# Neighbourhood attention with tokens by grid column, and hand-overs between engines reordered, in a two-block transformer kernel

## The reference, cut to what matters

```python
x = x + g1 * o_lat                                            # layers 0 and 1
x = x + g2 * swiglu(modulate(rms_norm(x, norm_gain[i, 1]), sh2, sc2), ffn_w_in[i], ffn_w_out[i])
...
y_mla = _mla(q_lat, kv_lat, k_pe, ...) * jax.nn.silu(g_mla)   # 8 heads
y_na = _na(na_q, na_k, na_v, ...) * jax.nn.silu(g_na)         # 16 heads of 64
h_res = h_res + jnp.concatenate([y_mla, y_na], axis=-1) @ w_out[l]
return h_res[:, N_META:]
# _na: a query sees all 4 rows of 16 columns around its own, and the 16 meta tokens
c0 = np.clip(cols - NA_WIN_C // 2, 0, GRID_W - NA_WIN_C)
bias = rel_bias[:, dr_idx[None, :, None], dc_idx[:, None, :]]
s = jnp.concatenate([s_win.reshape(B, NA_HEADS, GRID_W, n_win), s_meta], axis=-1)
p = jax.nn.softmax(s, axis=-1)
```

## Time and profile before

| | us |
|---|---|
| runs | 1249.21, 1249.61, 1250.48 |
| median | 1249.61 |
| profiled execution | 1249.41 |
| its span in the trace | 1247.7 |

### The profile page before, as it was taken

The page is one execution under the profiler, slowest core; times in us unless marked ns, Lnnn a source line. Parts: engine busy times, 40 slices in busy tenths (PEclk is TensorE's granted clock), DMA queues, the critical chain, the costliest instruction groups (busy, mean ns, idle before and its releaser), DMA issues.

```text
span 1247.7 us, 18627 instructions
## 1 busy us (share of the span) xinstructions
PE 1187.5 (95%) x7096; PEld 983.6 (79%) x7096; DVE 704.2 (56%) x1174; ACT 542.4 (43%) x1002; POOL 86.4 (7%) x124
## 2 busy tenths in 40 slices
PE   7999999999999999899989989999989999999898
PEld 5765787787788887578965889999979885998466
DVE  3544576767623334667679564445576465445753
ACT  3234422222222323544358554445455675565752
POOL 0002011122100000100000200000010000200400
PEclk9999999999999999899999999999999999999999
DMA  9889455677632233122330245555535341653110
GB/s 327 305 304 324 138 164 174 201 265 247 231 101 76 94 101 101 35 100 74 130 102 1 70 156 180 188 182 171 174 102 160 130 135 35 155 174 135 35 65 37
DMA packets 121510, 183.32 MB, mean 147 GB/s; under 512 B 4321, under 2 KB 92688, under 8 KB 121440
## 3 DMA queue, kind: packets, MB, share of 16 engines
q1 hardware_dynamic: 113888, 154.64, 37.1%
q0 software_dynamic: 7552, 27.73, 7.1%
HBM read 181.31 MB, written 1.05 MB: 146 GB/s over the span
## 4 chain that ended last, share of the span: by engine, by line
PE 82%; DVE 8%; ACT 4%; issue 3%; POOL 1%; DMA 0%; DVEq 0%; SPq 0%; ACTq 0%; POOLq 0%
PE ps L464 20%; PE ps L466 20%; PE ps L465 20%; PE ps L794 2%; PE ps L796 2%; PE ps L795 2%; PE ps L835 2%; PE ps L2097 1%; PE ps L2141 1%; PE ps L2429 1%; PE ps L2431 1%; PE ps L2430 1%; PE ps L1274 1%; ACT wh L442 1%; DVE wl L449 1%
## 5 line engine op out<-in xcount | busy, mean ns | idle before, releaser
L449 DVE TENSOR_TENSOR wl<-raw,wh 128x1024 fp32r<-128x1024 f32 (+1 forms) x246 | 295.4, 1206 | 248.2 <-ACT wh L442 245.3
L464 PE MATMUL ps<-hh,wh 128*128 128x256 f32 (+2 forms) x1256 | 419.6, 334 | 13.5 <-DVE hl L594 8.3
L465 PE MATMUL ps<-hl,wh 128*128 128x256 f32 (+2 forms) x1256 | 410.3, 327 | 0.0
L466 PE MATMUL ps<-hh,wl 128*128 128x256 f32 (+2 forms) x1256 | 409.3, 326 | 0.0
L442 ACT ACTIVATE wh<-raw 128x1024 fp32r<-128x1024 f32 (+1 forms) x246 | 252.4, 1031 | 274.5 <-PE ps L466 256.2
L464 PEld LDWEIGHTS ps<-hh,wh 128*128 128x128 f32 x1256 | 238.1, 190 | 54.8 <-issue 24.8
L465 PEld LDWEIGHTS ps<-hl,wh 128*128 128x128 f32 x1256 | 237.5, 189 | 22.2 <-issue 1.9
L466 PEld LDWEIGHTS ps<-hh,wl 128*128 128x128 f32 x1256 | 238.3, 190 | 20.9
L464 PE MATMUL ps<-ah,wh 128*128 128x256 f32 (+2 forms) x392 | 131.9, 336 | 3.7 <-DVE al L1927 3.0
L465 PE MATMUL ps<-al,wh 128*128 128x256 f32 (+2 forms) x392 | 129.6, 331 | 0.0
L466 PE MATMUL ps<-ah,wl 128*128 128x256 f32 (+2 forms) x392 | 129.5, 330 | 0.0
(11 more groups left out here) (224 smaller groups left out, 1424.0 us busy)
## 6 DMA issues: line engine op xcount, KB each, us to landing
raw<-in_ffn_w_in SPq DMA_DIRECT2D x44, 1024.0 KB, 5.1
raw<-in_ffn_w_out SPq DMA_DIRECT2D x22, 1024.0 KB, 4.9
raw<-in_w_in SPq DMA_DIRECT2D x22, 1024.0 KB, 5.4
big<-in_w_ada SPq DMA_DIRECT2D x16, 1024.0 KB, 9.4
big<-in_w_ada POOLq DMA_DIRECT2D x24, 512.0 KB, 4.4
ex<-in_w_ada POOLq DMA_DIRECT2D x24, 512.0 KB, 4.9
raw<-in_diff_w_in SPq DMA_DIRECT2D x12, 1024.0 KB, 5.1
raw<-in_w_out SPq DMA_DIRECT2D x8, 1024.0 KB, 4.9
```

The lines of the kernel that those rows point to most:

```text
L449: ins = nc.vector.tensor_tensor(place(wl), v, place(wh).bitcast(F32), ALU.subtract)
L464: nc.tensor.matmul(o, w_hi, m_hi, start=first, stop=False, **kw)
L465: nc.tensor.matmul(o, w_hi, m_lo, start=False, stop=False, **kw)
L466: return nc.tensor.matmul(o, w_lo, m_hi, start=False, stop=last, **kw)
```

## The change

**Order of tokens.** Tokens are reordered by grid column (column by column, 4 tokens each). The copies of x and ctx from PSUM and the copies, roundings and splits around the Fourier mixer's output write every fourth word (`by_column`). The position tables, the mask and the output DMA follow that order.

**Neighbourhood attention.** 128 queries are now 32 columns, and their windows lie in 40 columns: 160 keys and 16 meta tokens. The first half of queries uses 176 columns, the second 192, of which 16 in the middle are a masked gap. Transposes per step are two of 128 columns and two of 48 or 64 (the side), in one bank. Values per pair of heads are one matmul per head for the side (112 rows, 256 queries) and one of 128 queries per head and half. POOL copies the side's rows of the values by DMA, in three parts. POOL's bias is two additions of 160 columns and one copy of meta columns per head, and its runs come in by four DMAs instead of two. Only one unit remains in step 2; the other value unit runs ahead of the loop.

**Out-projection.** The latent part (k 0 to 7) is computed as eight blocks (`latent_part`, 12 matmuls each, in bank 7) that DVE adds to `x_tok` (`latent_added`): six inside the loop (steps 5 to 12, 17, 18, 19), two behind. The remaining halves are k 8 to 15. Halves of the weights are rounded in steps 2, 3, 13 to 16, and split one step later.

**Elsewhere.** In `ffn_out` the last tile goes to `hh[:, 0]`/`hl[:, 0]` right after tile 20. In the differential attention the roundings of `last_unit` move to step 16, the splits to step 17. In `units_dve` a head is rotated directly behind its own norm and not one unit later. Gathered squares are 4 instead of 6 for `"ffn1"` and `"second"`. In `MLA_UNITS` the unit `ahead` stands behind all of `b`. Gate units rotate over banks 0 and 1 only, the sums of `"lat"` are in banks 2 and 3, and `x_tok` is copied by DVE alone, inside the gate units.

The diff, cut to its core:

```diff
-SLOTS_R = 2 * ROWS - 2
-RUN = REL_C * (SLOTS_R - 1) + GRID_W
-RUNS_AT = 6400
-BIAS_W = N_META + SLOTS_R * GRID_W + N_META
+NEAR_C = GRID_W // 2 + NA_WIN_C // 2
+NEAR = NEAR_C * ROWS
+SIDE_C = GRID_W - NEAR_C
+SHIFT_C = GRID_W // 2 - SIDE_C
+RUN = REL_C * (ROWS - 1) + NEAR_C + SHIFT_C
+RUNS_AT = 2048
+KEYS = (NEAR + N_META, 2 * N_META + NEAR)
+KEYS_AT = (0, NEAR)
+KEYS_W = 2 * NEAR + 2 * N_META
...
+        def by_column(tokens):
+            if tokens.shape[-1] == L:
+                return tokens.rearrange("p (c r) -> p r c", r=ROWS)
+            return tokens.rearrange("p (s c r) -> p s r c", r=ROWS, c=GRID_W)
...
+                "second": [(0, 0, L2)], "lat": [(2, 0, L), (3, L, HW)]}
+
+        GATHERED = {"ffn0": KD - 2, "diff": KD - 2, "ffn1": KD - 4, "second": KD - 4}
...
-                MLA_UNITS += a[:1] + [second] + a[1:2] + [third] + a[2:] + b[:2] + ahead + b[2:]
+                MLA_UNITS += a[:1] + [second] + a[1:2] + [third] + a[2:] + b + ahead
...
-                                 out=[seg(nkx[:, m, 0:N_META], L, L2),
-                                      seg(nkx[:, m, N_META:N_META + L2], 0, L2)]))
+                                 out=[seg(nkx[:, m, NEAR:NEAR + N_META], L, L2), seg(nkx[:, m, 0:NEAR], 0, NEAR),
+                                      seg(nkx[:, m, NEAR + 2 * N_META:], L - NEAR, L)]))
...
-            banks = (0, 1, 2, 5, 6, 7) if phase is MLA_UNITS else (0, 1, 2)
+            banks = (0, 1, 2, 5, 6, 7) if phase is MLA_UNITS else (0, 1) if phase is GATE_UNITS else (0, 1, 2)
...
-                if i > lag and phase[i - lag - 1].get("rope"):
-                    u = phase[i - lag - 1]
+                if i >= lag and phase[i - lag].get("rope"):
+                    u = phase[i - lag]
...
-                    last_unit()
+                    units_act(act, link, last_unit, False)
+                if i == a["steps"]:
+                    round_next(act, last_unit[0]["q"] - 1, 2)
...
             for i in range(a["steps"] + 10):
-                if i == 2:
-                    last_unit()
+                if i == a["steps"] + 1:
+                    split_next(dve, last_unit[0]["q"] - 1, 2)
```

```diff
+        OUT_Q = 2 * G["out2"]
+        PART_AT = {}
+        for x in range(8):
+            PART_AT.setdefault(5 + x, []).append(divmod(x, 2))
+        PART_AT.update({17: [(4, 0)], 18: [(4, 1)], 19: [(5, 0), (5, 1)]})
+        PARTS_IN = 6
+        ROUND_AT = {2: [-2], 3: [-1], 13: [0], 14: [1], 15: [2], 16: [3]}
+
+        def latent_part(pe, g, half):
+
+            turn, b = divmod(g, 4)
+            t, c = divmod(b, 2)
+            if g and not half:
+                pe.wait_ge(s_part, g)
+            for k in range(4 * turn + 2 * half, 4 * turn + 2 * half + 2):
+                q = OUT_Q + k
+                if b == 0:
+                    pe.wait_ge(split, q + 1)
+                n = slice(c * 512, (c + 1) * 512)
+                at = L2 + t * P
+                w_h, w_l = wh[:, q % SPLIT_SLOTS, n], wl[:, q % SPLIT_SLOTS, n]
+                a_h, a_l = hh[:, k, at:at + P], hl[:, k, at:at + P]
+                nc.tensor.matmul(ps[:, 7, :], a_h, w_h, start=(k == 4 * turn), stop=False)
+                nc.tensor.matmul(ps[:, 7, :], a_h, w_l, start=False, stop=False)
+                ins = nc.tensor.matmul(ps[:, 7, :], a_l, w_h, start=False, stop=(k == 4 * turn + 3))
+                if b == 3:
+                    ins.then_inc(used, 1)
+            if half and b < 3:
+                ins.then_inc(s_fill, 1)
+
+        def latent_added(dve, g):
+
+            turn, b = divmod(g, 4)
+            if b == 3:
+                dve.wait_ge(used, OUT_Q + 4 * turn + 4)
+            else:
+                dve.wait_ge(s_fill, 3 * turn + b + 1)
+            if turn:
+                dve.wait_ge(s_part, g - 3)
+            tile = x_tok[:, b // 2, b % 2 * 512:(b % 2 + 1) * 512]
+            nc.vector.tensor_tensor(tile, ps[:, 7, :], tile, ALU.add).then_inc(s_part, 1)
+
         def na_pe(pe, tail):
...
                 if 2 <= i < NA_STEPS + 2:
                     j0 = i - 2
-                    main, meta = (0, L) if j0 % 2 == 0 else (N_META, 0)
+                    main, side, n = (0, P, 48) if j0 % 2 == 0 else (64, 0, 64)
                     pe.wait_ge(s_w, NA_S0 + j0 + 1)
                     if j0 == 1:
...
+                    pe.wait_ge(s_side, 96 if f < 6 else 144)
                     if f >= 1:
                         pe.wait_ge(s_on, NA_G0 + f)
-                    for j, n in enumerate((P, P, N_META)):
+                    head = [slice((2 * f + c) * NA_DIM, (2 * f + c + 1) * NA_DIM) for c in range(2)]
+                    for c in range(2):
+                        nc.tensor.matmul(ps[64 * c:64 * c + 64, 6, 0:L], nv_side(slice(0, 112), head[c].start, NA_DIM),
+                                         wTs[0:112, c, :], start=True, stop=False, skip_group_check=True)
+                    for t in range(2):
+                        q = slice(t * P, (t + 1) * P)
                         for c in range(2):
-                            ins = nc.tensor.matmul(ps[64 * c:64 * c + 64, 6, 0:L], nv_of(j, (2 * f + c) * NA_DIM, NA_DIM),
-                                                   wT3[0:n, c, j, :], start=(j == 0), stop=(j == 2))
+                            ins = nc.tensor.matmul(ps[64 * c:64 * c + 64, 6, q], nv_real[:, t, head[c]], wTn[:, c, q],
+                                                   start=False, stop=(t == 1), skip_group_check=True)
                     ins.then_inc(s_pv, 1)
-                if 2 <= i < NA_STEPS + 2:
-                    if j0 >= 1:
-                        pe.wait_ge(s_trc, NA_S0 + j0)
-                    for c in range(2):
-                        ins = nc.tensor.transpose(ps[0:N_META, 7, c * P:(c + 1) * P],
-                                                  ex3[:, j0 % 3, c, meta:meta + N_META], T["ident"])
-                    ins.then_inc(s_tr, 1)
+                for g, half in PART_AT.get(i, ()):
+                    latent_part(pe, g, half)
                 tail(i)
 
         def na_act(act, link):
 
             for i in range(NA_STEPS + 5):
                 if i == 2:
-                    units_act(act, link, NA_UNITS[-2:])
+                    units_act(act, link, NA_UNITS[-1:], False)
                 if i < NA_STEPS:
+                    n = KEYS[i % 2]
                     for c in range(2):
                         act.wait_ge(s_mx, na_max_done(i) - 1 + c)
```

```diff
+                for g in range(PARTS_IN):
+                    if (g, 1) in PART_AT.get(i - 1, ()):
+                        latent_added(dve, g)
                 if i < NA_STEPS:
                     f, t = divmod(i, 2)
...
+
+                pool.dma_start(nv_side(slice(32, 64), at, n), nv_real[96:P, 0, at:at + n]).then_inc(s_side, 16)
+                pool.dma_start(nv_side(slice(64, 96), at, n), nv_real[0:32, 1, at:at + n]).then_inc(s_side, 16)
+                pool.dma_start(nv_side(slice(96, 96 + N_META), at, n), nv_side(slice(0, N_META), at, n))\
+                    .then_inc(s_side, 16)
+
+            pool.wait_ge(s_ucp, na_v[2][2]["c"] + 1)
+            side_values(0, 512)
+            side_values(512, 256)
             pool.wait_ge(s_on, ATT["mla"]["g0"] + ATT["mla"]["groups"])
+            nc.gpsimd.memset(nkx[:, :, NEAR + N_META:NEAR + 2 * N_META], 0.0).then_inc(s_gap, 1)
...
+            pool.wait_ge(s_runs, 16 * ROWS)
             for h in range(NA_HEADS):
                 s = h % 4
                 if h >= 4 and h % 2 == 0:
                     pool.wait_ge(s_mx, na_max_done(h - 3))
-                at = RUNS_AT + (NA_HEADS - 1 - h) * RUN + RUN - 1
-                run = bass.AP(tensor=big, offset=at, ap=[[13824, P], [-REL_C, SLOTS_R], [-1, GRID_W]])
-                mask = bass.AP(tensor=tab, offset=sum(list(TABLE_COLS.values())[:N_KEPT - 1]), ap=[[KEPT, P], [0, SLOTS_R], [1, GRID_W]])
-                for c in (0, N_META + SLOTS_R * GRID_W):
-                    nc.gpsimd.tensor_copy(bias[:, s, c:c + N_META], meta_b[:, h * N_META:(h + 1) * N_META])
-                nc.gpsimd.tensor_tensor(
-                    bias[:, s, N_META:N_META + SLOTS_R * GRID_W].rearrange("p (j c) -> p j c", j=SLOTS_R),
-                    run, mask, ALU.add).then_inc(s_bias, 1)
+                if h == 8:
+                    pool.wait_ge(s_ucp, NA_UNITS[-1]["c"] + 1)
+                    side_values(768, 256)
+                nc.gpsimd.tensor_copy(bias[:, s, NEAR:NEAR + N_META], meta_b[:, h * N_META:(h + 1) * N_META])
+                for t in range(2):
+                    at = RUNS_AT + (NA_HEADS - 1 - h) * RUN + REL_C * (ROWS - 1) + NEAR_C - 1 + t * SHIFT_C
+                    run = bass.AP(tensor=big, offset=at, ap=[[13824, P], [-1, NEAR_C], [-REL_C, ROWS]])
+                    mask = bass.AP(tensor=tab, offset=sum(list(TABLE_COLS.values())[:N_KEPT - 1]) + t * NEAR_C,
+                                   ap=[[KEPT, P], [1, NEAR_C], [0, ROWS]])
+                    to = t * (NEAR + 2 * N_META)
```

(34 more changed lines are left out.)

202 lines of the change are left out of this document (107 added, 95 removed).

## The result

| | before | after |
|---|---|---|
| runs with the change first timed (us) | 1248.91 to 1250.48 | 1238.10, 1238.14, 1241.64, 1242.85, 1244.39 |
| median (us) | 1249.31 | 1241.64 |
| profiled execution, its span (us) | 1249.41, 1247.7 | 1238.10, 1236.4 |
| ratio of medians, 95% interval | | 0.9927 (0.9912 to 0.9942) |

The changed kernel is 0.7% faster: 7.7 us in the medians and 11.3 in the profiled executions, where 20.1 was forecast. The time lies above the range of the prediction. The four under 1240 have a mean granted clock of 0.992, the seven from 1241.3 up have 0.984 to 0.987. In the comparison of those six the kernel before stays at 1248.1 to 1252.1, ten of eleven executions at 0.990 or 0.991.

What follows compares the result with a forecast made beforehand. The prediction took TensorE (PE) to bound the kernel, busy 1187.5 of 1247.7 us, with idle time in holes at stage hand-overs. Its terms, -15.0 -2.5 -1.3 -2.6 -0.8 -1.7 +0 +3.5 +0.3, summed to -20.1: 1229 us, range 1221 to 1238.

Steps and rivals of the forecast that it cites:

- Attention and out-projection: Neighbourhood attention and out-projection: 97.3 us become 82.3, by 10.5 less work and waits from 11.9 to 7.4; -15.0 (-19 to -9).
- Second norm: Norm before the second block: fewer squares added by POOL end PE's 2.05 us wait earlier; -0.8 (-1.5 to +0.3).
- gates: Gate units: two banks instead of three add a 3.2 us hole and a half clock behind it; +3.5 (0 to +3.6).
- Norm of the second FFN: Norm before the second feed-forward block: it has no wait for POOL's squares like the second block's norm; 0.
- Strided order: Copies, roundings and splits writing every fourth word for the new token order; +0.3, bounded by 0 and 2.2 us.
- Latent units: Latent units: 0.95 won without DVE's copies of x, about 1.0 lost to rotation ahead of two splits; 0 (-0.95 to +1.0).
- ends of the FFNs: End of both feed-forward blocks: last tile rounded into a free buffer, so PE's low-part waits vanish; -2.5 (-2.6 to -1.0).
- step 2 of the differential attention: Differential attention: two splits ahead of DVE's weights move to steps 16 and 17, cutting PE's 3.88 us wait; -2.7, about -0.2 clock.
- (1): Attention loop: latent matmuls are not free; steps 5 to 16 take 3.6 us instead of 3.0, +7, giving 1236; chance 0.17.
- (2): Outside the attention: waits only move, 8.9 us given back, giving 1238; chance 0.05.
- (3): Gates and loop: the gate wait triggers no clock fall and the loop hides DVE's splits, -6, giving 1223; chance 0.13.
- (4): Attention loop: POOL's bias build becomes the bound, binding from 1.3 us per addition; slower than before, 1252 at 2.3; chance 0.03.

Runs made afterwards that it cites:

- b2_no_fill: The changed kernel with no latent products inside the attention loop, all of the out-projection behind it; median 1236.96 us, ratio to the kernel before 0.9893.
- a2_squares: The changed kernel with POOL adding six gathered squares again for both later norms, as before; median 1240.66 us, ratio to the kernel before 0.9914.
- b4_gates3: The changed kernel with gate units on three banks, latent norm's sums left where the change has them; median 1235.72 us, ratio to the kernel before 0.9880.
- c3_lat_late: The changed kernel with three gate banks, six gathered squares, no latent products in the loop, late rotation in the latent units; median 1228.40 us, ratio 0.9822.
- b3_attention: The changed kernel with only its token order, attention and out-projection kept, edits elsewhere undone; median 1241.83 us, ratio to the kernel before 0.9929.

## Why the prediction was off, by its own steps

**Attention and out-projection, -15.0, measured -11.4.** The step that failed is the balance of before: I took the whole of the 97.3 that was not work by my rows, 11.9, for waits, and let 4.5 of them vanish. The list of waits has 7.8 in that stage before and 8.0 after, so nothing was won there; all of the 11.4 is work, which fell from 90.2 to 78.9 (forecast 10.5 less). The work that I had put at 85.4 was priced too low: the pairs by 3.0, of which a half clock from 1161.1 to 1164.4 is 1.7; the out-projection by 1.0; the two units and their sum by 0.8. The out-projection is a misreading of the earlier trace rows: that window ends at 1242.6, before the last matmuls do. Read to their end, 180 of them take 41.7 us and not 41.0:

```profile
1201.60:1243.40 41.80, 41.73 (x182) 33.76 (x180) 17.29 (x18) 13.04 (x13) 0.00 (x0) 1.00 0.14 51
```

Second comes the price of a latent matmul. I took 0.228 from that row. A long row costs 0.232, and the 96 latent ones take 25.1 us, 0.262 each, 3.2 more than priced: 0.266 in the bursts of six between small matmuls, 0.254 in the blocks of twelve behind which PE waits for the bank. The first of a burst takes 0.32 to 0.34 in the rows above (1162.34 to 1162.67 for one). Third is what the fill is for: I credited it with covering waits that the narrower keys remove by themselves. The price of the keys was right (3.05 against 3.20 per pair), and b2_no_fill shows that they alone bring the stage to -15.1 (98.3 to 83.2, to the end of the last matmul), by chance the number forecast.

**Second norm, -0.8, measured +2.4.** I read that POOL would be done earlier and did not place the sum in PE's own order. With four gathered squares it stands after the sixth of eight product blocks, and PE works in order: 1.3 us. I named what was queued behind the wait in the gates, and not here. The half clock behind the wait, which I left out as well, then falls on the queued products, 1.3 more. Before, it fell on the transposes of x, behind which PE has to wait for DVE in any case (1.28 in a2_squares without the half clock, 0.03 before with it).

**Norm of the second FFN, 0, measured +1.5.** "No such wait" was right, but two more sums cost PE 0.6 where it is dense (a2_squares). The rest, 0.9, is the half clock at the hole of 3.1, which lasts 6.8 us here and 3.4 before; a2_squares and b4_gates3, with the same hole, have 3.4 again, so this part goes by the execution.

**Strided order, +0.3, measured +1.7.** The bounds held, the choice between them did not: the writes cost 1.3. The splits last 1.09, over the 0.9 that the prediction set as the sign of this.

**Latent units, 0, measured +0.2.** Right, and by its own parts: 0.95 was to be won and 1.0 lost. Before, PE waits here for the normalised head, and after it does not:

```profile
935.52 0.36 PE L464 MATMUL ps<-hh,wh 128*128 128x272 f32 x1 [0.95 <-DVE nrm L893]
```

That is 1.1 won, and 1.3 are lost, since DVE's rotation now stands in front of four splits:

```profile
931.78 1.82 DVE L936 TENSOR_TENSOR ex<-nrm,tab 32x272 f32<-32x272 f32 x4
...
935.10 4.63 DVE L474 TENSOR_TENSOR wl<-raw,wh 128x1024 fp32r<-128x1024 f32 x4
...
936.38 0.39 PE L489 MATMUL ps<-hh,wh 128*128 128x272 f32 x1 [1.21 <-DVE wl L474]
```

PE waits 1.21 for the split. c3_lat_late confirms the cause and shows that the loss was not the price of the gain: the copies of x, which are gone from here, had made the old wait.

**Also right within 0.5:** ends of the FFNs (-2.7 for -2.5), rotation (-1.4 for -1.3), step 2 of the differential attention (-3.1 for -2.6), MLA (-1.8 for -1.7), gates (+3.5 for +3.5). In the rows of after the first scores start with no wait, and the weights' wait is 1.18, as the prediction's test for a hole at 645 said:

```profile
635.40 1.99 PE L995 MATMUL ps<-big 64*128 64x512 f32 x8
...
644.31 0.66 PE L1022 MATMUL ps<-tab,big 128*128 128x128 f32 x4 [1.18 <-DVE big L1119]
```

**Rivals.** (1), the loop doesn't take the latent matmuls for free, at 1236: steps 5 to 12 took 3.1 each and not 3.6, so POOL did not do it, but the weights' slots and the bank made the fill a loss all the same. (2), the waits elsewhere only move, at 1238, has the number nearest to the profiled 1238.1, and that is luck: of its five terms four were won (9.0 for 8.1), and only the second norm's 0.8 was given back. (3) is out, as the clock did fall in the gates (0.53 at 950.4). (4) is out, as POOL's addition takes

```profile
L1676 POOL TENSOR_TENSOR big<-big,tab 128x160 f32<-128x160 f32 x32 | 21.5, 691 | 0.0
```

0.69 us, far from the 1.3 from which it would bind. The estimate from the row was 0.5. With the +50% that the Trainium skill ("GPSIMD Engine Reference", section "7. Performance pitfalls for Q7 kernels") puts on a read step over 8 bytes, the estimate was 0.8; the measured time lies between the two.

**The clock.** The range was built on one profiled execution and on a kernel whose runs had agreed within 0.2%. It had no term for a change after which the clock itself varies. The median lies 3.6 us above the profiled execution for it, of the 12.6 between 1229 and 1241.6.

## What to carry over

Before filling an engine's waits in a loop, first take out what another part of the same change removes: b2_no_fill shows that narrower keys left two waits of 0.5 us together per pair to fill, while the fill brought weights, banks and additions with it. For each wait that is moved, read the queue of the engine that waits: a wait of 2 us for the same sum cost 1.3 us more in the middle of a row of products than at its end, and another 1.3 where the clock fell behind it. And take a stage's removable waits from the list of waits, not from the stage's length minus the work that one has priced; and see that a window ends where its work does.

## What was not expected of the hardware

Writes with a step of four words cost ACT 1.87 times and DVE 1.47 to 1.57 times the contiguous ones. Matmuls of 128x512 in bursts of six between small ones cost 0.266 instead of 0.232 each. And the granted clock fell to half in executions at places where it did not in others that run the same code there, behind holes of 1.1 to 1.5 us: near 702 in seven of thirteen profiles, at 1157 and 1195 in a2_squares and at 1194 in b3_attention, none of these in the changed kernel's profiled executions. In the trace of the kernel before, the smallest hole with a half clock behind it is the 2.05 of the second norm, and its 1.5 us near 702 has none.
